# 32 bytes of padding behind the small buffers of a two-block transformer kernel on one Trainium2 core

## The reference

```python
shift, scale, gate = jnp.split(jax.nn.silu(c) @ w_mod + b_mod, 3, axis=-1)   # layers 0 and 1
hx = _rmsnorm(x, norm_w) * (1 + scale[:, None]) + shift[:, None]
a_h, a_b, a_c, a_z, q, k, v, r_z = _split_in(hx @ w_in)                      # 2048 -> 8192
...
x = x + gate[:, None] * (jnp.concatenate([y_conv, y_ret], axis=-1) @ w_out)  # 2048 -> 2048
...
proj = h @ w_in[i]                                                           # 2048 -> 6144
x = x + rms_norm(o @ w_out[i], ln_mix_post[i])
g, u = jnp.split(h @ w_gate_up[i], 2, axis=-1)                               # 2048 -> 11264
f = (jax.nn.silu(g) * u) @ w_down[i]                                         # 5632 -> 2048
gate = jax.nn.sigmoid(rms_norm(x, ln_pli[i]) @ w_pli_gate[i])
x = x + gate * (p[i] @ w_pli_proj[i])
```

## The kernel before

| line | stationary, modulo 128 | moving, modulo 128 |
|---|---|---|
| L1817 | `w_hi`, `w_lo`: 0 | `act`, `h`: 96 |
| L1824 | `act`, `quarters`, `f`, `h`: 96 | `w_hi`, `w_lo`: 0 |
| L2063 | `a_hi`, `a_lo`: 96 | `act`: 96 |

## Time and profile before

### The profile page before, as it was taken

How to read it: one execution, slowest core, us unless ns; L and a number is a source line. 1 busy time by engine, 2 the same in 40 slices (tenths; PEclk the granted TensorE clock), 3 DMA queues, 4 the chain that set the end, 5 groups by cost and what they waited for, 6 DMA issues and landing times.

```text
span 2968.4 us, 45132 instructions
## 1 busy us (share of the span) xinstructions
PE 2913.9 (98%) x16565; PEld 2545.5 (86%) x16565; DVE 1827.9 (62%) x2354; ACT 1346.8 (45%) x1875; POOL 119.6 (4%) x129
## 2 busy tenths in 40 slices
PE   7899999999999999999999999999999999999999
PEld 4678887788888889998888899998999999988877
DVE  6868788878775346654446666665655555544464
ACT  6732222343443235444445577675544444434353
POOL 0000000010110000000011100000000000000000
PEclk9999999999999999999999999999999999999999
DMA  7855555444554226543334655555455555565554
GB/s 282 296 195 187 182 184 183 156 154 167 182 205 171 97 89 201 183 148 110 110 114 139 182 164 171 163 161 191 157 184 184 184 185 181 189 201 189 187 176 161
DMA packets 144750, 515.28 MB, mean 174 GB/s; under 512 B 16753, under 2 KB 16793, under 8 KB 142721
## 3 DMA queue, kind: packets, MB, share of 16 engines
q1 hardware_dynamic: 141264, 495.01, 50.6%
q0 software_dynamic: 3376, 18.77, 1.8%
HBM read 511.49 MB, written 2.22 MB: 173 GB/s over the span
## 4 chain that ended last, share of the span: by engine, by line
PE 91%; DVE 3%; ACT 2%; issue 2%; DMA 2%; DVEq 0%; ACTq 0%; POOL 0%; SPq 0%
PE main L1824 52%; PE main L1817 33%; PE aux L1776 2%; DVE w_lo L1104 1%; DMA raw<-in_w_mod 1%; PE aux L1977 1%; PE aux L1968 1%; ACT w_hi L626 1%; PE aux L2044 0%; PE aux L2028 0%; PE main L2192 0%; PE aux L2081 0%; PE aux L1980 0%; ACT u L934 0%; PE aux L1971 0%
## 5 line engine op out<-in xcount | busy, mean ns | idle before, releaser
L1104 DVE TENSOR_TENSOR w_lo<-raw,w_hi 128x1024 fp32r<-128x1024 f32 (+1 forms) x836 | 1012.3, 1212 | 859.0 <-ACT w_hi L626 850.1
L626 ACT ACTIVATE w_hi<-raw 128x1024 fp32r<-128x1024 f32 (+1 forms) x836 | 858.9, 1031 | 1267.3 <-PE main L1824 728.1
L1824 PE MATMUL main<-w_hi,act_hi 128*128 128x512 f32 (+1 forms) x1408 | 535.9, 381 | 2.9 <-DVE scores L1328 1.5
L1824 PE MATMUL main<-w_lo,act_hi 128*128 128x512 f32 (+1 forms) x1408 | 526.7, 374 | 0.0
L1824 PE MATMUL main<-w_hi,act_lo 128*128 128x512 f32 (+1 forms) x1408 | 526.7, 374 | 0.0
L1817 PE MATMUL main<-h_hi,w_hi 128*128 128x256 f32 x1408 | 395.9, 281 | 1.1 <-DVE h_lo L1250 1.1
L1817 PE MATMUL main<-h_hi,w_lo 128*128 128x256 f32 x1408 | 395.6, 281 | 0.0
L1817 PE MATMUL main<-h_lo,w_hi 128*128 128x256 f32 x1408 | 395.6, 281 | 0.0
L1824 PE MATMUL main<-w_hi,quarters 128*128 128x384 f32 (+1 forms) x1280 | 360.0, 353 | 0.0
L1817 PE MATMUL main<-act_hi,w_hi 128*128 128x256 f32 (+1 forms) x960 | 322.4, 336 | 2.4 <-DVE act_lo L1207 1.4
L1817 PE MATMUL main<-act_hi,w_lo 128*128 128x256 f32 (+1 forms) x960 | 321.0, 334 | 0.0
(11 more groups left out here) (307 smaller groups left out, 3296.5 us busy)
## 6 DMA issues: line engine op xcount, KB each, us to landing
raw<-in_w_ffn_up SPq DMA_DIRECT2D x176, 512.0 KB, 3.8
gates<-in_w_side SPq DMA_DIRECT2D x128, 512.0 KB, 3.5
raw<-in_w_in_ret SPq DMA_DIRECT2D x128, 512.0 KB, 4.1
raw<-in_w_in_conv SPq DMA_DIRECT2D x120, 512.0 KB, 4.1
raw<-in_w_out SPq DMA_DIRECT2D x96, 512.0 KB, 3.5
raw<-in_w_ffn_down SPq DMA_DIRECT2D x88, 512.0 KB, 3.6
raw<-in_w_mod SPq DMA_DIRECT2D x64, 512.0 KB, 4.6
raw<-in_w_sb SPq DMA_DIRECT2D x64, 384.0 KB, 3.3
```

The lines of the kernel that those rows point to most:

```text
L626: A(w_hi[:, slot, 0:w], raw[:, slot, 0:w], ACT.Copy).then_inc(hi_split, 1)
L1104: V.tensor_tensor(out=w_lo[:, slot, 0:w], in0=raw[:, slot, 0:w], in1=w_hi[:, slot, 0:w].bitcast(F32), op=ALU.subtract).then_inc(lo_split, 1)
L1824: ins = mm(bank[:, c0:c1], x, w_part[:, slot, j * n + c0:j * n + c1], start=(k == 0 and j == 0 and i == 0), stop=(k == per - 1 and j == 1 ...
```

## The change

`sum_fin` is declared with 16 columns instead of 8, of which the first two are used as before. It takes 64 bytes instead of 32, and every buffer declared after it lies 32 bytes higher.

```diff
         mix_a = sb(top, "mix_a", [P, KT])
         ssq_fin = sb(top, "ssq_fin", [P, 2, 4])
-        sum_fin = sb(top, "sum_fin", [P, 8])[:, 0:2]
+        sum_fin = sb(top, "sum_fin", [P, 16])[:, 0:2]
         act_hi = sb(layer, "act_hi", [P, KT * 512], F32R)
```

## The result

The changed kernel takes 2944.61 us (median of 4 runs, 2941.75 to 2948.21) against 2971.43 (4 runs, 2969.5 to 2972.63) of the kernel before: ratio 0.9912, 95% interval 0.99 to 0.9924. It is 0.9% faster, where 2.7% was forecast. The profiled execution's span fell by 25.5 us, from 2968.4 to 2942.9, at a mean granted clock of 0.995 against 0.997.

What follows compares the result with a forecast made beforehand. TensorE's time from one matmul's start to the next was taken to bound the kernel. Terms of 43.7, 28.8, 2.6 and 5.4 us made 80.5 us less, forecasting 2892 us (-2.7%), range 2800 to 2977.

Steps and rivals of the forecast that it cites:

- TensorE alone sets the time: Whole kernel: TensorE busy 98% of the span, so the change acts only through the time between matmul starts.
- A's mechanism: L1817 and L1824: operands alike modulo 512 run at L2063's 0.4427 ns a column; 80.5 us less, 2892 us; chance 0.50.
- The test named for it: L2063 in its stretch without `mod0`: staying at 226.7 ns would show that the distance between operands counts.
- The 512-column term: L1817 and L1824: 6624 matmuls fall from 233.3 to 226.7 ns, 43.7 us less.
- The 256-column terms: 118.3 (L1817) and 116.7 ns (L1824) fall to 113.3: 28.8 and 2.6 us less.
- the 384s: L1824: 1536 matmuls of 384 columns fall from 173.5 to 170.0 ns, 5.4 us less.
- The bound: 256- and 384-column terms: at worst only the 512s gain, 43.7 us in all; at best the sum is 111.8 us.
- C: Rival: only the moving operand's beginning counts; L1817's 256 columns gain 9.2 us, 2963 us; chance 0.08.
- D: Rival: no effect, L2063's rate has another cause; 2972 us; chance 0.14.
- B: Rival: both operands at 0 are better still, about 215 ns for 512 columns; 198 us less, 2774 us; chance 0.12.
- E: Rival: each operand's place counts by itself, 96 the better; 240.0 ns for 512 columns at (0, 0); 3039 us; chance 0.16.
- The costs taken as nothing: VectorE's and ScalarE's work on moved buffers, transposes and new waits on TensorE: 0, up to 5 us left to the range.

Runs made afterwards that it cites:

- experiment 1: Standalone sheet: rows of 96 matmuls for 38 pairs of columns and operand beginnings; equal pairs 226.9 ns at 512 columns, 120 at 256; no kernel time.
- experiment 5: Standalone sheet: moving operand at 0, stationary at each 32 bytes to 480, plus loads of 32 and 64 columns; 226.7 to 234.3 ns at 512 columns.
- Experiment 8: Standalone sheet: rows of 48 matmuls, 8 pairs of columns and distance, each behind 8 different short rows; 256 columns at distance 64: 113.3 or 117.8 ns.
- `h_plus64`: Changed kernel with `h` moved so that the distance in `ffn_up` is 64 bytes; 2916.92 us, ratio 0.9822 to the kernel before.
- `pad64`: `sum_fin` declared with 24 columns where the changed kernel has 16, later buffers 32 bytes higher than there; 2961.52 us, ratio 0.9971 to the kernel before.
- `pad128`: `sum_fin` declared with 40 columns where the changed kernel has 16, later buffers 96 bytes higher than there; 2986.07 us (one run).
- `h_plus32`: Changed kernel with `h` moved back to the earlier distance of 32 bytes in `ffn_up`; 2940.38 us, ratio 0.9902 to the kernel before.
- `pad96`: `sum_fin` declared with 32 columns where the changed kernel has 16, later buffers 64 bytes higher than there; 2960.78 us, ratio 0.9967 to the kernel before.
- `both_plus64`: `h` moved to distance 64 in `ffn_up`, and layer 1's activations and `quarters` moved too; 2908.74 us, ratio 0.9818 to the kernel before.

## Why the prediction was right in sign and wrong in size

**TensorE alone sets the time, and only the step from start to start can change it.** Right: same counts, the same waits, and the classes' 26.0 us beside the span's 25.5.

**A's mechanism.** Right, and shown by experiments 1 and 5: the distance between the operands decides, and equal operands are best for 512 columns, wherever they lie. The test named for it came out: L2063 is at 226.7 in both kernels. The prediction counts distances modulo 128; the period is 256 (experiment 5). That did not touch this forecast, since the change makes the operands alike modulo 512. Why the distance acts it called a reading, and that is still open.

**The 512-column term.** 43.7 forecast, 36.9 measured. The settled step is 226.7 as taken, but in stages where other matmuls stand between the pieces it takes a while to settle: behind the transposes of L1776 the second to seventh step average 229 to 234 ns. So L1824's 3456 matmuls on `act` average 227.7 even without the steps that reach over an interruption, and their sum went from 821.1 to 804.4 us, 16.7 less instead of 22.8: 6.1 of the 6.8 us that were missing. Experiment 8 shows the same: 48 matmuls of 512 columns at distance 0 take 11.01 us up to the next kind when they follow eight fp32 matmuls (317.13 to 328.14 in its timeline) and 10.88 when they follow four of 512 columns.

**The 256-column terms: here the prediction failed.** The step that failed is "I take the same share a column, since in L1824 today 256 columns cost exactly half of 512". Forecast 31.4 us less, measured 11.3 us more: 42.7 of the 54.5 us by which the sum was off (512 columns: 6.8; 384: 5.0). What two equal operands have on top of one cycle a column is 13.3 ns a matmul at each of these widths, not 0.026 ns a column (0.4427 - 0.4167), so 256 columns cost 120.0 and not 113.3. The half was an accident of distance 224, where the rest on top is 20.0 ns at 512 columns and 10.0 at 256. The rows in hand spoke against a share: the same distance has 13.5 ns at 384 columns (173.5 - 160) and not the 15 halfway between 20 and 10, and in L1817 118.3 is not half of 233.3. From the earlier trace rows the 384s already had the 13.3 ns of L2063, so that a fixed rest would have foretold no gain there. With it the forecast would have been 43.7 less, 5760 x 1.7 + 768 x 3.3 = 12.3 more: 31 us less, against 25.5 measured.

**The bound.** "From below by nothing" left out that two equal operands can be worse than unequal ones. So A's own range (2860 to 2933) missed 2944.6; the whole range held it only because the rivals C and D were in it.

**The rivals.** B falls: both at 0 is no better than both at 96. C and E fall by experiment 1. D falls by the result and by each of the experiments. The Trainium skill (TensorE: Matmul & The Clock Gate, "Wait — 56ns, not 53.3ns?") gives 215.7 ns for 512 columns. No run here agrees: no row of the kernels or of the sheets settles under 226.7 for these float32r matmuls with a load each, and the distance moves it up to 234.3. For this case the measurement decides.

**The costs taken as nothing.** Right: VectorE's mean for `w_lo` is 1213 ns against 1212 before, ScalarE's 1031 in both; TensorE's idle time in the span is 57.1 us against 54.5.

**What stays open.** Why the distance counts, and what picks one of the two steps that 256 columns have at 64 and 192. That the reads of load and moving columns get in each other's way is the prediction's reading. The narrow loads speak for some part of the load in it (256 columns at distance 0: 120.0 to 113.3 ns) and against a simple share (512 columns at distance 0: 226.7 to 231.7), and no run took the loads away at equal columns. Why the distance acts is not shown; that it acts is.

## What to carry to other kernels

When a matmul with its own load sets the time, measure its step from start to start as a function of the distance between its two operands, for each width that the kernel uses, before moving a buffer: the best distance here was 0 for 512 columns and 64 for 256, and a padding that gives all of them the same one gave back 11 of 37 us. (Distance 16, tried in the first sheet in one direction, had 226.7 and 118.3; no run puts it into the kernel.) Check the step in the kernel itself, too: the gain of `h_plus64` rests on one long stretch that settled at 113.3, and nothing found here makes sure that it does. A price per item that is known at one width should be split into a fixed and a growing part from rows of at least two widths at the same place, and a term that no row shows needs a bound on the side of loss too.

## What was not expected of the hardware

- Distance between the operands modulo 256 bytes moves a float32r matmul by up to 3.4% (226.7 to 234.3 ns at 512 columns) and 5.9% (113.3 to 120.0 at 256); 16 bytes cost nothing at 512 columns (226.7) and gave 118.3 at 256.
- The same 48 matmuls on the same operands hold one of two steps, 113.3 or 117.8 ns, from row to row. What picks the step was not found.
- Narrower loads can make the step shorter or longer: 256 columns at distance 0 cost 113.3 ns with 32 columns loaded and 120.0 with 128, 512 columns at distance 32 cost 240.0 and 233.3.
- After the same wait for `act_lo` the granted clock is sometimes lower. The changed kernel, and the window of the kernel before under it:

```profile
157.43 0.63 PE L2063 MATMUL main<-act_hi,a_hi 128*128 128x512 f32 x1 [2.11 <-DVE act_lo L1608]
157.86 0.63 PE L2063 MATMUL main<-act_hi,a_lo 128*128 128x512 f32 x1
...
152.00:164.00 12.00, 9.89 (x39) 7.72 (x39) 8.79 (x13) 7.76 (x10) 0.00 (x0) 0.86 0.15 54
```

```profile
157.63 0.50 PE L2063 MATMUL main<-act_hi,a_hi 128*128 128x512 f32 x1 [2.10 <-DVE act_lo L1608]
...
152.00:164.00 12.00, 9.90 (x46) 7.78 (x45) 8.78 (x13) 7.77 (x10) 0.00 (x0) 1.00 0.17 56
```

Behind a wait of 2.1 us in both, the matmuls of the first are 427 ns apart, twice the usual: 1.2 GHz. It lasts for nine of them and costs the 2 us by which L2063 takes longer after the change. `pad64`, `pad128` and `h_plus32` show 0.86 in the same window, `pad96`, `h_plus64` and `both_plus64` 1.00, and `h_plus64` has these buffers where the changed kernel has them, so it doesn't go with the placement that was changed.
